# Hybrid attention layer on eight cores: Q and K of each head in seven half products, V made transposed and turned, two heads of buffers

## The reference

```
proj = x @ w_in                      # 2048 x 19456: q, k, v (3072 each), u, c_gate, b_gate (2048 each), g_attn, g_conv
for g, (window, dilation) in enumerate(((128, 1), (512, 4), (2048, 16))):   # 8 heads of 128 in each group
    outs[g], lses[g] = dilated_band_attention(q[g], k[g], v[g], window, dilation)
mix_w = softmax(stack(lses), axis=0)
attn = sum(mix_w * outs) @ w_attn_o
conv = (b_gate * causal_short_conv(c_gate * u, conv_w)) @ w_conv_o
merged = (sigmoid(g_attn) * attn + sigmoid(g_conv) * conv) @ w_out
x = layer_norm(ALPHA * x + merged)
x = layer_norm(ALPHA * x + (silu(x @ w_ffn_gate) * (x @ w_ffn_up)) @ w_ffn_down)
```

## Time and profile before

| | us |
|---|---|
| median of 3 runs (4447.37 to 4602.51) | 4452.4 |
| the profiled execution | 4449.98 |
| its span on the slowest core (core 1) | 4448.4 |
| spans of the 8 cores | 4438.4 to 4448.4 |
| PE busy in that span | 4396.3 |
| DVE busy | 2338.5 |
| ACT busy | 626.8 |
| attention stage, about | 113.7 to 1264 |

### The profile page before, as it was taken

How to read it: one execution, slowest core, us unless ns; L and a number is a source line. 1 busy time by engine, 2 the same in 40 slices (tenths; PEclk the granted TensorE clock), 3 DMA queues, 4 the chain that set the end, 5 groups by cost and what they waited for, 6 DMA issues and landing times.

```text
span 4448.4 us, 68110 instructions; the slowest of 8 cores (4438.4 to 4448.4 us)
## 1 busy us (share of the span) xinstructions
PE 4396.3 (99%) x26160; PEld 2254.0 (51%) x26160; DVE 2338.5 (53%) x3468; ACT 626.8 (14%) x1042; POOL 290.9 (7%) x549
## 2 busy tenths in 40 slices
PE   7999999999999999999999999999999999999998
PEld 4666666666644444444444444444444444444443
DVE  0355455544576533367666365666333466574465
ACT  0111111111111111041001011111111221010011
POOL 2000000000000000000000001000000000000000
PEclk9999999999999999999999999999999999999999
DMA  9566676666245544735545458644444645554454
GB/s 130 109 135 139 147 159 139 147 143 150 53 121 157 142 119 118 151 79 90 96 87 90 72 90 160 176 152 155 124 117 114 142 79 87 96 90 81 81 96 131
DMA packets 162831, 527.70 MB, mean 119 GB/s; under 512 B 16464, under 2 KB 28752, under 8 KB 159824
## 3 DMA queue, kind: packets, MB, share of 16 engines
q0 software_dynamic: 85824, 278.96, 38.5%
q1 hardware_dynamic: 76688, 244.39, 16.2%
HBM read 715.43 MB, written 86.77 MB: 180 GB/s over the span
## 4 chain that ended last, share of the span: by engine, by line
PE 96%; DMA 2%; issue 1%; DVE 1%; another core or an unknown queue 1%; POOL 0%; ACT 0%; DVEq 0%; POOLq 0%; ACTq 0%
PE pb L358 96%; DMA arena<-w_ffn_down 1%; DMA arena<-x_t 1%; DVE arena L367 0%; PE pb L361 0%; DVE arena L376 0%; POOL arena L124 0%; DMA slabs<-w_ffn_up 0%; ACT arena L364 0%; POOL slabs L124 0%; DVE slabs L367 0%; DVE arena L383 0%; DVE small L1003 0%; DVE tmps L376 0%
## 5 line engine op out<-in xcount | busy, mean ns | idle before, releaser
L358 PE MATMUL pb<-arena,slabs 128*128 128x512 bf16 x14120 | 3082.0, 379 | 27.3 <-DMA arena<-x_t 24.5
L358 PEld LDWEIGHTS pb<-arena,slabs 128*128 128x128 bf16 x14120 | 1381.7, 98 | 1668.8 <-issue 36.8
L358 PE MATMUL pb<-slabs,arena 128*128 128x128 bf16 (+1 forms) x9152 | 1042.7, 273 | 2.3 <-DMA slabs<-w_ffn_down 2.2
L358 PEld LDWEIGHTS pb<-slabs,arena 128*128 128x128 bf16 x9152 | 655.1, 113 | 358.5 <-issue 4.6
L367 DVE TENSOR_TENSOR arena<-pb,arena 128x512 f32<-128x512 f32 (+1 forms) x569 | 436.6, 778 | 429.4 <-PE pb L358 423.9
L367 DVE TENSOR_TENSOR arena<-arena,pb 128x512 f32<-128x512 f32 x555 | 381.1, 687 | 473.7 <-PE pb L358 469.3
L364 ACT ACTIVATE arena<-pb 128x512 f32<-128x512 f32 (+2 forms) x443 | 260.0, 587 | 2478.1 <-PE pb L358 1287.6
L358 PE MATMUL pb<-arena 128*128 128x128 bf16 (+1 forms) x2032 | 374.9, 307 | 8.9 <-DVE arena L376 6.7
L355 DVE CAST arena<-pb 128x512 bf16<-128x512 f32 x144 | 99.5, 691 | 539.7 <-PE pb L358 539.6
L367 DVE TENSOR_TENSOR slabs<-slabs 128x2048 bf16<-128x2048 bf16 (+1 forms) x336 | 261.9, 820 | 10.4 <-DMA slabs<-w_ffn_up 1.5
L358 PEld LDWEIGHTS pb<-arena 128*128 128x128 bf16 x2032 | 189.4, 103 | 141.9 <-issue 16.9
(11 more groups left out here) (61 smaller groups left out, 986.1 us busy)
## 6 DMA issues: line engine op xcount, KB each, us to landing
slabs<-w_sums SPq DMA_DIRECT2D x213, 512.0 KB, 5.4
slabs<-w_in POOLq DMA_DIRECT2D x90, 512.0 KB, 13.6
slabs<-w_ffn_gate POOLq DMA_DIRECT2D x88, 512.0 KB, 6.0
slabs<-w_ffn_up POOLq DMA_DIRECT2D x88, 512.0 KB, 5.9
slabs<-w_ffn_down POOLq DMA_DIRECT2D x78, 512.0 KB, 7.1
w_sums<-tmps SPq DMA_DIRECT2D x73, 512.0 KB, 5.2
arena<-w_in POOLq DMA_DIRECT2D x38, 512.0 KB, 8.4
w_sums<-arena SPq DMA_DIRECT2D x38, 512.0 KB, 3.9
```

The lines of the kernel that those rows point to most:

```text
L358: sch.op("pe", lambda e: e.matmul(out, lhsT, rhs, start=start, stop=stop, skip_group_check=onto), reads, writes)
```

## The change

Heads 0 and 1 are projected as before. For heads 2 to 23:

- Q and K of two blocks of 512 tokens come from seven products of 8 matmuls (`prod`), with q's weights as a and k's as b, twice per head (p = 0 for tokens 0 to 1023, p = 1 for the rest). In each half DVE joins with six operations of 128x512 that read a bank in PSUM and float32 in SBUF (`vtt`, after M5, M1, M2, M3, M6 and M7), and ACT copies three times (after M4, M2 and M3).
- The sums of the two weight blocks are made by DVE in `sums0` to `sums2`, in the steps of the head before, from weights loaded a head ahead.
- The x sums of both halves (`RA`) are made once, at the start. S4 and S3 overwrite the x blocks B21 and B12. What still needs plain x (V, the conv groups of the last head) uses the overwritten blocks with summed weights.
- V comes from 4 groups of 16 matmuls of 128x512, with the weights as the stationary operand (`v_turned`), so it comes out transposed; ACT writes it to SBUF and 16 PE transposes per head (`v_turn`), four at a time in bank 5, turn it; ACT copies it back.
- Two heads of buffers: the attention of head i runs between the pieces of **head i + 1** (`plan`).
- Banks: sums of attention in 0, 1, 2; scores in 4 alone; products in 3, 6, 7 in turn; V in 5.
- With dilation 1 ACT copies the attention sums, not DVE.
- `fin` writes to NUM in place and each result is stored to `attn_keep`, in HBM; both halves are read back later.
- `prep_steps` has one set of `raw` in place of two, and five steps per pair: `diff`, `own`, `cross` (whose end issues the loads of the next pair), and two that do nothing. It starts in head 1's steps and ends in head 21's.
- NCONV[0] is 2 in place of 4: the mixer of the first half takes blocks 2 and 3 in seven products too.

```diff
-    P_ACC = (0, 1, 2, 3)
-    P_S = (4, 5)
-    P_PROJ = (6, 7)
+    P_ACC = (0, 1, 2)
+    P_S = (4,)
+    P_PROJ = (3, 5, 6, 7)
...
+    qb3 = {"n": (3, 6, 7)}
...
-        sl = i % 3
+        sl = i % 2
...
+        def sums0():
+            a, b = W0[(i, "q")], W0[(i, "k")]
+            c = pst["c"] = Slab(None, 2)
+            vtt(c.view, a.view, b.view, ALU.subtract, [a.buf, b.buf], [c.buf])
+            vtt(a.view[:, 1024:2048], a.view[:, 0:1024], a.view[:, 1024:2048], ALU.add, [a.buf], [a.buf])
+
+        def sums1():
+            a, b = W0[(i, "q")], W0[(i, "k")]
+            vtt(s1v, a.view[:, 0:1024], b.view[:, 1024:2048], ALU.add, [a.buf, b.buf], [B_half[0]])
+            vtt(b.view[:, 0:1024], b.view[:, 0:1024], b.view[:, 1024:2048], ALU.add, [b.buf], [b.buf])
+
+        def sums2():
+            v = W0[(i, "v")]
+            vtt(svv, v.view[:, 0:1024], v.view[:, 1024:2048], ALU.add, [v.buf], [B_half[1]])
...
+        def prod(p, nm):
+            a, b, c = W0[(i, "q")], W0[(i, "k")], pst["c"]
+            if nm == "M4":
+                qb3["n"] = (qb3["n"][1], qb3["n"][2], qb3["n"][0])
+                for k, n in zip("UVX", qb3["n"]):
+                    pst[k] = banks[n], bank_bufs[n]
+            w, bw, k0, r, z, fresh = {
+                "M4": (b.view, b.buf, 8, "S4", "U", True), "M5": (a.view, a.buf, 8, "B22", "V", True),
+                "M1": (s1v, B_half[0], 0, "S1", "X", True), "M2": (b.view, b.buf, 0, "B11", "U", False),
+                "M3": (a.view, a.buf, 0, "S3", "V", False), "M6": (c.view, c.buf, 0, "S6", "X", True),
+                "M7": (c.view, c.buf, 8, "S7", "U", True)}[nm]
+            bk, bb = pst[z]
+            for kc in range(8):
+                r_, c_ = RA[p][r].at(kc)
+                mm(bk[:, :], w[:, (k0 + kc) * 128:(k0 + kc + 1) * 128], r_, fresh and kc == 0, kc == 7,
+                   [bw] + c_, [bb], not fresh)
+            dv, bd = (tmps[:, 6, 0:512], [B_tmp[6]]) if p == 0 else (vf(QD, 512), cl(QD, 2 * KB))
+            ev, be = vf(QE, 512), cl(QE, 2 * KB)
+            t0, t1 = 1024 * p, 1024 * p + 512
+            if nm == "M4":
+                act(dv, bk[:, :], AF.Copy, [bb], bd)
+            elif nm == "M5":
+                vtt(dv, dv, bk[:, :], ALU.subtract, [bb] + bd, bd)
+            elif nm == "M1":
+                vtt(dv, dv, bk[:, :], ALU.add, [bb] + bd, bd)
+            elif nm == "M2":
+                act(kT[:, t0:t0 + 512], bk[:, :], AF.Copy, [bb], [ck[2 * p]])
+                vtt(ev, dv, bk[:, :], ALU.subtract, [bb] + bd, be)
+            elif nm == "M3":
+                act(qT[:, t1:t1 + 512], bk[:, :], AF.Copy, [bb], [cq[2 * p + 1]])
+                vtt(ev, ev, bk[:, :], ALU.add, [bb] + be, be)
+            elif nm == "M6":
+                vtt(kT[:, t1:t1 + 512], ev, bk[:, :], ALU.subtract, [bb] + be, [ck[2 * p + 1]])
+            else:
+                vtt(qT[:, t0:t0 + 512], dv, bk[:, :], ALU.add, [bb] + bd, [cq[2 * p]])
+                a.used()
+                b.used()
+                c.used()
...
+        def v_turned(tt):
+
+            p, odd = divmod(tt, 2)
+            v = W0[(i, "v")]
+            bk, bb = banks[5], bank_bufs[5]
+            for kc in range(16):
+                lo, k = kc < 8, kc % 8
+                r_, c_ = RA[p][("B11", "S3")[odd] if lo else ("S4", "B22")[odd]].at(k)
+                if lo != bool(odd):
+                    w, bw = svv[:, k * 128:(k + 1) * 128], B_half[1]
+                else:
+                    w, bw = v.view[:, kc * 128:(kc + 1) * 128], v.buf
+                mm(bk[:, :], w, r_, kc == 0, kc == 15, [bw] + c_, [bb])
...
+            act(dst, src_, AF.Copy, [bb], cv)
+
+        def v_turn(b4):
+
+            bk, bb = banks[5], bank_bufs[5]
+            bkb = bk[:, :].bitcast(BF16)
+            blocks = [4 * j + b4 for j in range(4)] if dil == 4 else [4 * b4 + j for j in range(4)]
+            for j, b in enumerate(blocks):
+                tp(bkb[:, j * 128:(j + 1) * 128], vsb[:, b, :], cv + [B_const], [bb])
+            dst = vsb[:, b4::4, :] if dil == 4 else vsb[:, 4 * b4:4 * b4 + 4, :]
+            act(dst, bkb[:, 0:512].rearrange("p (b d) -> p b d", b=4), AF.Copy, [bb], cv)
+
+        def plan(nxt):
+
+            P = lambda p, nm: (8, lambda: prod(p, nm))
+            V = lambda tt: (16, lambda: v_turned(tt))
+            T = lambda b4: (2, lambda: v_turn(b4))
+            if dil == 16:
+                t1, t2 = [], [T(0), T(1), T(2), T(3)]
+            else:
+                t1, t2 = [T(0), T(2), T(1)], [None, T(3), None, None]
+            N = [(0, f_) for f_ in nxt] + [None] * (3 - len(nxt))
+            seq = [P(0, "M4"), P(0, "M5"), P(0, "M1"), V(0), P(0, "M2"), t1[0] if t1 else None, P(0, "M3"), V(2),
+                   P(0, "M6"), t1[1] if t1 else None, P(0, "M7"), V(1), P(1, "M4"), t1[2] if t1 else None, P(1, "M5"),
+                   V(3), P(1, "M1"), t2[0], P(1, "M2"), N[0], t2[1], P(1, "M3"), N[1], t2[2], P(1, "M6"), N[2], t2[3],
+                   P(1, "M7")]
+            return [x for x in seq if x is not None]
...
-                            vcp(A[:, j * 512:(j + 1) * 512], tbk[:, :], [tbb], cA[2 * j:2 * j + 2])
+                            act(A[:, j * 512:(j + 1) * 512], tbk[:, :], AF.Copy, [tbb], cA[2 * j:2 * j + 2])
...
-                    o, co = attn_ap(h, 256 * qd, 256)
-                    vtt(o, num[:, cs], den[:, cs], ALU.mult, cn + cd, co)
+                    o = vb(NUM + qd * KB, 256)
+                    vtt(o, num[:, cs], den[:, cs], ALU.mult, cn + cd, cn)
+                    o0 = h * 1024 + 256 * (qd % 4)
+                    sch.dma("sp", S_keep[qd % 4], at_d[qd // 4][:, o0:o0 + 256], o, reads=cn, writes=[B_keep])
...
-    NCONV = (4, 2)
+    NCONV = (2, 2)
...
+            def own():
+                vtt(a[:, 1024:2048], a[:, 0:1024], a[:, 1024:2048], ALU.add, c_a, c_a)
+                keep(1, a, c_a, 0)
+                vtt(b[:, 0:1024], b[:, 0:1024], b[:, 1024:2048], ALU.add, c_b, c_b)
+                keep(2, b, c_b, 2048)
 
             def cross():
-                vtt(hh, a[:, 0:1024], b[:, 1024:2048], ALU.add, ca + cb, [ch])
-                keep(1 + n % 2, hh, [ch], 6144)
-                if 1 <= n and n + 1 < len(PAIRS):
+                vtt(sum_c[:, 0:1024], a[:, 0:1024], b[:, 1024:2048], ALU.add, c_a + c_b, c_c)
+                keep(3, sum_c[:, 0:1024], c_c, 6144)
+                if n + 1 < len(PAIRS):
                     load(n + 1)
 
-            def own_a():
-                vtt(a[:, 1024:2048], a[:, 0:1024], a[:, 1024:2048], ALU.add, ca, ca)
-                keep(3, a, ca, 0)
-
-            def own_b():
-                vtt(b[:, 0:1024], b[:, 0:1024], b[:, 1024:2048], ALU.add, cb, cb)
-                keep(4, b, cb, 2048)
-
-            return [diff, cross, own_a, own_b]
-
-        out = [lambda: (load(0), load(1))]
+            def rest():
+                pass
+
+            return [diff, own, cross, rest, rest]
...
+    for f_ in combsA[0]:
+        f_()
...
+    for f_ in combsA[1]:
+        f_()
...
-        if i + 2 < 24:
-            P_ = heads[i + 2][0] + heads[i + 2][1] + heads[i + 2][2]
+        if i + 1 < 24:
+            P_ = heads[i + 1][3](heads[i + 2][4] if i + 2 < 24 else [])
         else:
-            P_ = [ucb0.pop(0) for _ in range(12)]
-        k = 0
+            P_ = [(16, ucb0.pop(0)) for _ in range(12)]
+        k, spent, total = 0, 0, sum(c for c, _ in P_)
         for si, a_ in enumerate(A_):
+            if i + 2 < 24 and si < 3:
+                first_weights(i + 2, "qkv"[si])
             a_()
             for f_ in prev_fins[:(len(prev_fins) + len(A_) - 1 - si) // (len(A_) - si)]:
                 prev_fins.pop(0)()
-            if 1 <= i < 21:
+            if i < 22:
                 seen += 1
                 while prep and len(prep) > prep_n - (prep_n * seen + slots - 1) // slots:
                     prep.pop(0)()
-            target = ((si + 1) * len(P_)) // len(A_)
-            while k < target:
-                P_[k]()
+            while k < len(P_) and (si == len(A_) - 1 or (spent + P_[k][0] / 2) * len(A_) <= (si + 1) * total):
+                P_[k][1]()
+                spent += P_[k][0]
                 k += 1
-                if i == 23 and k in (2, 5, 8, 11):
...```

**Order of instructions, PE**, where the attention of head 4 (dilation 4) ends and that of head 5 begins. pb0 to pb3 are sums of attention, pb4 (and pb5 before) scores. Before, pb6 and pb7 get V of head 6 in 64 small matmuls each, and the last row is Q of head 7:

```order
L358 MATMUL pb2<-arena 128x128 x2
L358 MATMUL pb3<-arena,ones 128x128 x2
L358 MATMUL pb6<-slabs,arena 128x128 x64
L358 MATMUL pb7<-slabs,arena 128x128 x64
L358 MATMUL pb4<-arena 128x128 x4
L358 MATMUL pb6<-arena,slabs 128x512 x16
```

156 lines of the change are left out of this document (96 added, 60 removed).

## The result

| | before | after |
|---|---|---|
| median, same chip | 4449.4 us | 4508.7 us |
| profiled execution | 4450.0 us | 4508.0 us |
| its span | 4448.4 us | 4506.4 us |
| PE busy | 4396.3 us | 4350.9 us |
| PE idle | 52.1 us | 155.5 us |

The changed kernel is 1.3% slower: the ratio is 1.0132, its 95% interval 1.0115 to 1.0149. The forecast was 4426 us, the range 4385 to 4485. The time lies outside it, on the other side of no change, though within 2%. In some executions the cores of one die, or of both, show a lower granted clock for the whole run; all times, ratios and profiles here are of executions and cores without that.

What follows compares the result with a forecast made beforehand. PE, busy 4396.3 of 4448.4 us, was taken as the bound. Work -84.7, head-end waits +41, pairs +15, first mask +3, mixer's start -1 sum to -26.7; 4450.0 - 26.7 + 2.4 for the median = 4426 us, range 4385 to 4485.

Steps and rivals of the forecast that it cites:

- work removed: PE matmuls saved: Q and K 76.1 us, V 3.4, conv 5.2; together 84.7 us less for PE.
- head 1's first mask: Second half's `RA` operations on DVE, ahead of head 1's attention, delay its first mask: +3 us, once (0 to 5).
- mixer's start and the rest: `RA`-like operations no longer stand at the mixer's start, where they caused a wait of 0.78 us: -1 us.
- Each wait that the change makes on PE costs in full: In attention, PE has no waits now for a new one to replace, so each costs its length.
- 24 x 0.2163 = 5.2 us: Conv, blocks 2 and 3 of the first half: 192 matmuls become 168, saving 5.2 us.
- head-end wait: Next head's scores wait for DVE's operation on M7, 22 times: 41 us, bounds 27 and 75.
- pairs' loads: `prep_steps`, one buffer set: DVE waits 85 us for loads at `diff`, 15 us reach PE, bounds 0 and 85.
- DVE keeps up: Heads of dilation 1: ACT does the copies, M7's operation starts with M7's end, PE waits 1.2 us.
- bare wait: At each head's end, PE waits 1.2 us for M7's operation even with DVE idle, 22 times.
- Rival 2: Single set of pair buffers governs; every `diff` finds its load missing: 85 in place of 15, 4496 us; chance 0.13.
- signs of being wrong: PE waiting in mid-head, waits ahead of scores over 4 us, or POOL's pair loads over a step late after `cross`.
- rival 4: V's transposes hold PE for their whole record of 219 ns, not 56: 57 us more, 4483 us; chance 0.01.

## Why the prediction was wrong

| term | forecast | measured in the trace of after |
|---|---|---|
| work removed | -84.7 | -84.7 (pitches unchanged) |
| waits at head ends and from the pairs | +41 + 15 | +71.8 at head starts, +4.2 inside heads |
| head 1's first mask | +3 | +2.7 |
| conv groups of the last head | 0 | +19.5 |
| mixer's start and the rest | -1 | +5.2 |
| lower granted clock | 0 | +39.3 |
| sum | -26.7 | +58.0 |

**The step that failed most: a wait was priced at its length.** "Each wait that the change makes on PE costs in full" was too little. The longest wait in the rows was 1.50 us, so a clock loss had neither a term nor a bound, and no rival had it, although waits of 2.3 to 3 us were in the forecast. The kernel before with waits of 2.47 and 3.27 us put in shows 1.4 and 2.0 us more for each. This is 39.3 of the 84.7 us between the two sums (by chance the same figure as the work). Without it the sum would be +18.7, some 4471 us: inside the range, still slower and not faster.

**The conv groups were costed for their matmuls alone.** "24 x 0.2163 = 5.2 us" was right, but the sum of the weight halves that makes this saving possible is in the diff, inside the step and directly ahead of its first matmul, so it waits for the slab's load and DVE, and PE for it. I gave it no wait and no bound: 19.5 us of waits, and 28 us of time, as the kernel with these sums ahead showed. The forecast said "hardly any elsewhere in attention".

**The head-end wait had its mechanism right and its sizes low.** That there would be 22 of them, ahead of the scores, held. In sum 76 us where 56 were forecast and 27 + 0 to 75 + 85 were its bounds. Set against the kernel without the pairs' loads, which had a term of their own, the 22 head starts are 60 us where 41 were forecast: 25.8 for 18.4 behind dilation 4, 18.7 for 14.0 behind dilation 16, and 15.8 for 8.4 behind dilation 1, where "DVE keeps up" was false. The pairs' loads bring these last to 26.8, with 6.57, 5.48 and 5.15 us the longest waits of all, so "longest in boundaries behind dilation 4" failed. Even the three quiet ones there are 1.68 us and not 1.2, since one sum stands ahead of M7's operation (0.60). The quiet ones behind dilation 16 are 2.13 us and behind dilation 4 mostly 3.41 to 3.67, where I had 2.0 and 2.3. The bare wait, 1.2 us in the forecast, is 1.05 in the kernel with early sums. Behind dilation 4 the queue was itself right, as this stretch of DVE up to PE's wait of 3.67 us at 485.16 shows:

```profile
480.60 2.03 DVE L367 TENSOR_TENSOR arena<-pb,arena 128x512 f32<-128x512 f32 x2
482.53 0.68 DVE L367 TENSOR_TENSOR tmps<-tmps 128x1024 bf16<-128x1024 bf16 x1
483.14 0.68 DVE L367 TENSOR_TENSOR arena<-arena,pb 128x512 bf16<-128x512 f32 x1
483.73 0.68 DVE L367 TENSOR_TENSOR slabs<-slabs 128x1024 bf16<-128x1024 bf16 x1
484.34 0.68 DVE L367 TENSOR_TENSOR arena<-arena,pb 128x512 bf16<-128x512 f32 x1
```

The operations lie at the pitches that I took, and the last ends at 485.02, but DVE came to the queue already late: M1's operation starts at 474.21 where the forecast's count, taken back from M7's end at 481.49, has it at about 473.1. A mask and the 2048 wide sum of `prep_steps` are ahead of it.

**The pairs' loads** were the small matter that I had taken them for: 15 us forecast, and in the kernel without them 11 us of time less and 15.1 us of waits on the slowest core (92.3 to 101.2 us of waits on the cores of the changed kernel, 86.0 to 86.9 there). That the size fits is partly luck, since the way was another. DVE waited 14.9 us for `tmps<-w_in` from 114 to 1220 us where I had up to 85, and a second way was written off with "Stores to `attn_keep` are 64 KB each: nothing". Both meet behind dilation 1. At the longest wait, 6.57 us at 279.5, DVE had stood for a pair's load with two sums of weights, M6's operation, another sum and M7's behind it:

```profile
274.86 1.23 DVE L367 TENSOR_TENSOR tmps<-tmps 128x2048 bf16<-128x2048 bf16 x1 [3.66 <-DMA tmps<-w_in]
```

Ahead of the 4.55 us at 434.1 it is a store:

```profile
419.32 2.07 ACT L364 ACTIVATE arena<-pb 128x512 f32<-128x512 f32 x4 [7.06 <-DMA attn_keep<-arena]
```

ACT's copy of the attention sums waits 7.06 us for the cells being stored, the exponentials queue behind it, and DVE's mask stands behind these. Ahead of the 5.48 and 5.15 us (728 and 880 us) both waits are there. Without the pairs' loads the four are 2.3 to 2.9 us. How the 11 us split between the two ways wasn't isolated. Rival 2 (4496 us) came nearest to the measured time for another reason: its chain of pairs isn't what governs the head ends.

Two of the signs of being wrong that the prediction named are there: six waits ahead of scores of over 4 us, and waits of PE in mid-head, though small, 4.2 us in all. The 2.4 us added for the median rest on three times of which one, 4602.5 us, is far off; without it they would be nothing, which changes no conclusion.

**What held.** PE's pitch of 128x512 is 0.2163 still, and the transposes, here four of them between two products, keep theirs, (573.75 - 573.53) / 4 = 0.055:

```profile
573.53 0.39 PE L361 MATMUL pb<-ident,arena 128*128 128x128 bf16 x4
573.75 1.89 PE L358 MATMUL pb<-arena,slabs 128*128 128x512 bf16 x8
```

So rival 4 fell; the Trainium skill (TensorE: Matmul & The Clock Gate, Part 4: PE-mode transpose), with some 275 ns for one, disagrees with these rows as with the earlier trace rows. DVE's busy time rose by 147 us (135 forecast), ACT was never the bound by its load, and the sign of "the work removed pays in full" was right: with half of the waits gone (50.0 us left) the same products run 0.5% faster than before.

## What to carry to other kernels

When PE is at 100% and full clock, a change that saves matmuls must be costed with two prices for every new wait, its length and the slow matmuls behind it: here, on average, 0.4 us for waits of 1.7 us, 1.4 for 2.5 and 2.0 for 3.3. An operation that is needed for the saving (a sum of weights, a difference) goes into the queue ahead of what PE waits for only if its place says so; walk the order of each engine backwards from each product that is read at once, in every stage that the diff touches and not only in the largest. Put the preparing operations behind a product that nobody reads soon, and give PE other work behind the last product; where that work shares a bank with what an engine still has to copy out, the wait comes back there (a bank of its own for it wasn't tried). An engine that "keeps up" on average is no argument for the few microseconds ahead of a wait: add up its queue there in each kind of head, with the transfers that stand in it.

## What the hardware showed that I had not expected

- The clock fell behind waits of 2.13 us and didn't behind others of 2.96 us in the same kernel; it fell at 2 of 22 waits of 1.68 us, at 18 of 22 of 2.47 and at all 22 of 3.27. The loss, where there was one, was mostly 1.7 us, what eight matmuls of 128x512 take more at 1.2 GHz (8 x 0.2163).
- Eight useless matmuls per head made a kernel some 14 us faster.
- Relaxing the order of stores changed nothing that can be measured, although ACT waits 7 us at a time for one of them; without the pairs' loads the same stores held ACT up for at most 1.9 us on any core.
